# A two-layer decoder trunk: low parts, norms, covers and an overflow body of PE rearranged

## The reference

```python
for l in range(DEPTH):                        # DEPTH = 2
    mod = (c_act @ ada_w[l] + ada_b[l]).reshape(bsz, 6, 1, D_MODEL)
    sh1, sc1, g1, sh2, sc2, g2 = (mod[:, i] for i in range(6))
    h = rms_norm(x, norm1_g[l]) * (1.0 + sc1) + sh1
    y = even_mixer(h, ...) if l % 2 == 0 else odd_mixer(h, ...)
    x = x + g1 * y
    h = rms_norm(x, norm2_g[l]) * (1.0 + sc2) + sh2
    x = x + g2 * grouped_moe(h, router_w, router_b, moe_w_gu[l], moe_w_down[l])
return rms_norm(x, final_g)
```

## Time and profile before

| | us |
|---|---|
| median of three runs | 891.27 (889.9 to 895.1) |
| the profiled execution, its own time | 894.63 |
| its span | 892.8 |
| PE busy | 810.5 (91%) |
| DVE busy | 329.5 (37%) |
| ACT busy | 166.6 (19%) |
| POOL busy | 26.0 (3%) |
| mean DMA rate over the span | 329 GB/s |

### The profile page before, as it was taken

How to read it: one execution, slowest core, us unless ns; L and a number is a source line. 1 busy time by engine, 2 the same in 40 slices (tenths; PEclk the granted TensorE clock), 3 DMA queues, 4 the chain that set the end, 5 groups by cost and what they waited for, 6 DMA issues and landing times.

```text
span 892.8 us, 12085 instructions
## 1 busy us (share of the span) xinstructions
PE 810.5 (91%) x5014; PEld 413.3 (46%) x5014; DVE 329.5 (37%) x815; ACT 166.6 (19%) x397; POOL 26.0 (3%) x65
## 2 busy tenths in 40 slices
PE   4899999899999999866999999898999999999864
PEld 2476444454333333222868778764454333332221
DVE  1188542472121111102789565535482111111102
ACT  2041231511111010002101333432421111010001
POOL 2000010110000000000000000000020000000000
PEclk9999999999999999988999999999999999999978
DMA  9999997687799999999999425202967799999993
GB/s 348 389 363 388 386 364 312 275 316 275 296 431 422 427 423 430 424 423 392 386 345 327 154 95 190 95 1 74 431 262 302 290 430 422 429 422 429 425 423 159
DMA packets 65116, 294.08 MB, mean 329 GB/s; under 512 B 2720, under 2 KB 3360, under 8 KB 49184
## 3 DMA queue, kind: packets, MB, share of 16 engines
q1 hardware_dynamic: 64352, 290.62, 82.1%
q10 hardware_dynamic: 560, 2.10, 0.6%
q0 software_dynamic: 144, 0.52, 0.2%
HBM read 292.18 MB, written 1.05 MB: 328 GB/s over the span
## 4 chain that ended last, share of the span: by engine, by line
PE 52%; issue 24%; DMA 12%; DVE 5%; ACT 3%; SPq 3%; POOL 0%; DVEq 0%; POOLq 0%; ACTq 0%
PE bank L847 13%; PE bank L843 11%; PE bank L1087 9%; DMA ring<-w_gu_dram 6%; PE bank L1109 4%; DMA ring<-w_down_dram 3%; DMA ring<-ada_w_dram 3%; PE bank L1073 3%; SPq L511 2%; PE bank L735 2%; PE bank L1124 2%; PE bank L694 2%; PE bank L759 1%; PE bank L914 1%; ACT tail L1287 1%
## 5 line engine op out<-in xcount | busy, mean ns | idle before, releaser
L1087 PE MATMUL bank<-ring,scr 128*64 128x512 f32 (+1 forms) x1024 | 193.8, 620 | 27.1 <-DMA ring<-w_gu_dram 14.7
L847 PE MATMUL bank<-hT,ring 128*128 128x256 f32 x640 | 142.1, 381 | 0.8 <-DVE hT L1634 0.8
L847 PEld LDWEIGHTS bank<-hT,ring 128*128 128x128 f32 x640 | 120.5, 190 | 18.4 <-issue 1.5
L1087 PEld LDWEIGHTS bank<-ring,scr 128*64 128x64 f32 (+1 forms) x1024 | 56.1, 130 | 151.7 <-issue 128.3
L1109 PE MATMUL bank<-ring,scr 128*64 128x512 f32 (+1 forms) x544 | 102.4, 597 | 1.4 <-DMA ring<-w_down_dram 1.0
L2059 DVE TENSOR_TENSOR hT<-bank,gb 128x512 f32<-128x512 f32 x28 | 19.4, 692 | 190.3 <-PE bank L1109 190.3
L843 PE MATMUL bank<-ring,xh 128*128 128x512 f32 x128 | 58.7, 612 | 0.7 <-ACT xh L1287 0.7
L843 PE MATMUL bank<-ring,hT 128*128 128x512 f32 x128 | 57.7, 607 | 0.1
L1472 ACT ACTIVATE scr<-bank 128x256 f32<-128x256 f32 (+1 forms) x42 | 19.1, 455 | 205.9 <-PE bank L1098 119.6
L1124 PE MATMUL bank<-hT,scr 64*128 64x512 f32 x224 | 55.6, 615 | 1.8 <-DVE hT L2059 1.8
L1109 PEld LDWEIGHTS bank<-ring,scr 128*64 128x64 f32 (+1 forms) x544 | 29.3, 127 | 59.8 <-issue 57.6
(11 more groups left out here) (252 smaller groups left out, 679.6 us busy)
## 6 DMA issues: line engine op xcount, KB each, us to landing
ring<-w_gu_dram SPq DMA_DIRECT2D x60, 2048.0 KB, 19.7
ring<-w_down_dram SPq DMA_DIRECT2D x28, 2048.0 KB, 17.5
ring<-ada_w_dram SPq DMA_DIRECT2D x24, 2048.0 KB, 15.9
ring<-od_w_in_dram SPq DMA_DIRECT2D x9, 2048.0 KB, 16.1
ring<-ev_w_in_dram SPq DMA_DIRECT2D x5, 2048.0 KB, 19.6
ring<-w_down_dram SPq DMA_DIRECT2D x8, 1024.0 KB, 27.3
scr<-w_gu_dram SPq DMA_DIRECT2D x10, 512.0 KB, 6.4
ring<-ev_w_out_dram SPq DMA_DIRECT2D x2, 2048.0 KB, 17.7
```

What stands on the lines that cost most here:

```text
L847: ins = pe.matmul(banks[h][:, m * 256:(m + 1) * 256], w[:, c, (2 * h + m) * P:(2 * h + m + 1) * P], x_part[:, c, :], start=(c == 0 and m = ...
L1087: ins = pe.matmul(b[o:o + r, :].rearrange("p (u f) -> p u f", u=2), h[:, c, r * i:r * i + r], wm, start=(first and c == 0), stop=(last and ...
```

## The change

Five edits.

- The low parts move from POOL to DVE, behind DVE's copy of `modp`. The copy of the router sums moves from DVE to ACT, behind the second high part; that high part moves in front of the exponential, and the first in front of ACT's rows of `hT`.
- The normalised rows are written in two halves of 512 columns on both engines, with a semaphore step for each; PE waits for the second half only in front of its third bank.
- In norms 1 to 3 DVE takes chunks 0, 1, 4, 5 (banks 0 and 2) and ACT chunks 2, 3, 6, 7 (banks 1 and 3).
- PE reads the flag before block 11 of the experts. The identity products are 5 and 7 in the routes, where they were 9 and 8. The four in front of the transposes of `ph` 2 are gone, and five stand behind the last scatter of layer 0, in front of the jump.
- The inside of PE's overflow body is a loop of four turns instead of four copies.

```diff
@@ gpsimd @@
-            def low_part(l):
-                for t in range(T):
-                    pool.wait_ge(hi_ready, 2 * l + t + 1)
-                    pool.tensor_tensor(by_chunks(x_lo[:, t, :]), by_fours(xh[:, t, :]),
-                          by_chunks(x_hi[:, t, :].bitcast(F32)), ALU.subtract)\
-                        .then_inc(lo_ready, 1)
-
             for n in range(5, 9):
                 root(n)
-                if n in (5, 8):
-                    low_part(n // 8)
@@ tensor, norm_T @@
-                if ph == 2:
-                    keep_busy(4, bank[0])
...
-                pe.wait_ge(xh_ready, ph + 1)
-                pe.wait_ge(xh_dve, ph + 1)
                 for b in range(4):
+                    if b % 2 == 0:
+                        pe.wait_ge(xh_ready, 2 * ph + b // 2 + 1)
+                        pe.wait_ge(xh_dve, 2 * ph + b // 2 + 1)
@@ tensor, fill @@
+                    if p == 0 and l == 0 and c >= 4:
+                        pe.wait_ge(hT_act, c - 3)
                     if p == 0 and l == 1 and c == 0:
-                        pe.wait_ge(hT_dve, 12)
-                    if p == 0 and c >= 4:
-                        pe.wait_ge(hT_act, 8 * l + c - 3)
+                        pe.wait_ge(hT_dve, 10)
+                        pe.wait_ge(hT_act, 10)
+                    if p == 0 and l == 1 and c >= 4:
+                        pe.wait_ge(hT_act if c // 2 % 2 else hT_dve, 8 + 2 * (c // 4) + c % 2 + 1)
@@ tensor, route @@
-                keep_busy(9 - l, bank[0])
+                keep_busy(5 + 2 * l, bank[0])
@@ tensor, experts @@
                 for b in range(BLOCKS):
+                    if b == BLOCKS - 3:
+                        pe.wait_ge(flag_ready, l + 1)
+                        over = pe.value_load(flag[0:1, l:l + 1])
...
                 scatter(BLOCKS - 1)
-
-            def overflow(l):
-                pe.wait_ge(flag_ready, l + 1)
-                over = pe.value_load(flag[0:1, l:l + 1])
+                if l == 0:
+                    keep_busy(5, bank[0])
+                return over
+
+            def overflow(l, over):
                 with pe.If(over > 0):
                     pe.wait_ge(tail_free, 4 * (l + 1))
                     with pe.Fori(0, POS) as e:
                         d = e * 28
-                        for q in range(4):
-                            pe.wait_ge(ov_dve[l], d + (7 * q + 2))
+                        with pe.Fori(0, 28, 7) as q:
+                            at = d + q
+                            pe.wait_ge(ov_dve[l], at + 2)
...
@@ scalar, norm @@
-                act.activation(xh[:, 0, :], xs[:, 0, :], ACT.Copy, scale=rstd[:, 0:1]).then_inc(xh_ready, 1)
+                for j in range(2):
+                    act.activation(xh[:, 0, j * W:(j + 1) * W], xs[:, 0, j * W:(j + 1) * W], ACT.Copy,
+                                   scale=rstd[:, 0:1]).then_inc(xh_ready, 1)
                 l, s = ph // 2, ph % 2
-                if ph == 1:
-                    row_out(2)
+                if s == 1:
+                    act.wait_ge(xh_ready, 2 * ph + 2)
+                    high_part(0)
                 act.wait_ge(x_ready, ph + 1)
-                for c in range(4, 8):
+                for c in ((2, 3, 6, 7) if ph else range(4, 8)):
...
                 if s == 1:
+                    if ph == 1:
+                        row_out(2)
+                    act.wait_ge(xh_dve, 2 * ph + 2)
+                    high_part(1)
+                    act.wait_ge(router_part, l + 1)
+                    act.activation(router_sum, bank[6][:, 0:2 * P], ACT.Copy).then_inc(router_out, 1)
 
                     act.activation(sm(895, 1), ones[:, 0:1], ACT.Exp)
-                    high_part(0)
@@ scalar, route @@
                 act.activation(pr, lg, ACT.Exp).then_inc(pr_ready, 1)
-                high_part(1)
@@ vector, tile_1, hT_rows and norm @@
-                dve.tensor_scalar(xh[:, 1, :], xs[:, 1, :], rstd[:, 1:2], None, ALU.mult).then_inc(xh_dve, 1)
+                for j in range(2):
+                    dve.tensor_scalar(xh[:, 1, j * W:(j + 1) * W], xs[:, 1, j * W:(j + 1) * W], rstd[:, 1:2], None,
+                                      ALU.mult).then_inc(xh_dve, 1)
...
-                for c in range(4):
+                for c in ((0, 1, 4, 5) if ph else range(4)):
...
                     dve.tensor_copy(modp[:, l, :], bank[6][:, 256:272]).then_inc(modp_out, 1)
-                    dve.wait_ge(router_part, l + 1)
-                    dve.tensor_copy(router_sum, bank[6][:, 0:2 * P]).then_inc(router_out, 1)
+                    for t in range(T):
+                        dve.wait_ge(hi_ready, 2 * l + t + 1)
+                        dve.tensor_tensor(by_chunks(x_lo[:, t, :]), by_fours(xh[:, t, :]),
+                          by_chunks(x_hi[:, t, :].bitcast(F32)), ALU.subtract)\
+                           .then_inc(lo_ready, 1)
```

16 lines of the change are left out of this document (8 added, 8 removed).

## The result

Over 15 runs each, the kernel before took 894.33 us and the changed one 887.03 us (medians). The ratio is 0.9917 with a 95% interval of 0.9895 to 0.9940, so the change takes off 7.4 us (5.4 to 9.4). One run of the kernel before took 1224.54 us, which doesn't move its median.

A forecast was written before the change was run, and what follows sets the result against it. PE (TensorE) was taken as the bound, busy 810.5 of 892.8 us, each gain carrying to the end. Border 7.1, route 0 2.6 and route 1 1.4 sum to 11.1: 891.3 to 880.2 us, range 875.5 to 886.5.

The forecast's parts named there:

- Border: Between the layers, norm 2: the first projection product starts 7.1 us sooner.
- a jump of 0.6: Border: PE's jump over the smaller overflow body costs 0.6 us, where a gap of 4.84 stood.
- 2.2 from transposes to projection: Norm 2: first transpose to first projection product takes 2.2 us instead of 2.76, as DVE and ScalarE share the chunks.
- The chosen reading: Border: the gap of 4.84 us comes from the overflow body's size; 184 instructions instead of 736 bring it to 0.6.
- the rival with 18%: Border: the jump keeps its 4.84 us, gain there about 1.5 instead of 7.1, time 885.8 us; chance 18%.
- Route 0: Route of layer 0: stall beside GpSimd gone, PE's shorter identity products end at 185.35 instead of 187.99, gain 2.6 us.
- the bound of -1.5: Route of layer 0: gain of -1.5 us if the adaLN row before the identity products is at half clock too.
- Route 1: Route of layer 1: DVE's stall of 2.87 us goes, first reduce 1.5 later, identity products covered; gain 1.4 us.
- its bound of 0.3: Route of layer 1: gain only 0.3 us if the clock loss of layer 0 occurs here.
- At nothing: Halves in norm 0, flag read before block 11 and layer 0's earlier front load: counted as no gain or loss.
- Slower rival: Routes and border: shortened identity products leave gathers and first projection at 1.2 GHz, together +11 us, 902 us; chance 3%.
- The stall's cause: Routes: GpSimd's low parts hold up tiny DVE operations, 5.24 us for two in layer 0; moving them removes it.

The follow-up runs named there:

- e2: Kernel before with only the border's edits (flag read ahead, five products behind the scatter, none before the transposes, body as a loop): 889.34 us, ratio 0.9950.
- e4: Changed kernel with the border edits taken back; halves, low parts on DVE and shorter covers stay: 894.85 us, ratio 1.0011.
- e9: Kernel before with only PE's flag read three blocks earlier; overflow body still written out four times: 892.16 us, one execution, against 893.61.
- e10: e9 with the overflow body as a loop over its four blocks: 890.38 us, one execution, against 893.61.
- e3: e2 with the overflow body written out four times, as in the kernel before: 888.53 us, ratio 0.9947.
- e5: Kernel before, unchanged, timed against itself and profiled a second time: 893.62 us against 893.01, ratio 0.9998.
- e1: Changed kernel with whole rows instead of halves in norm 0: 885.83 us against 893.33 for the kernel before, ratio 0.9925.
- e16: Changed kernel, unchanged, profiled a third time: 887.58 us, one execution, against 893.94 for the kernel before.
- e13: Changed kernel with five identity products in route 0 and four instead of seven in route 1: ratio a little under the expected 0.989 to 0.991.
- e11: Changed kernel with one and four identity products in the routes instead of five and seven; route 1 took 19.05 us, layer 0's experts lost 5.3.
- e12: e8 with one and four identity products in the routes instead of five and seven; experts of layer 0 took 232.24 us.
- e14: Changed kernel with three and four identity products in the routes instead of five and seven: ratio 0.4% under the changed kernel's 0.9917; route 0 took 21.71 us.
- e8: Changed kernel with the low parts on GpSimd again, each as soon as its high part is there: 886.49 us against 893.01, ratio 0.9928.

## Why the prediction was right at the border and failed in the routes

**Border: right by the stages.** The forecast was 7.1 us, the stages show 7.3 in the mean (5.9 to 8.5, by which profile of before is taken) and 7.38 in the two first profiles. By timing, these edits alone give 4.5 (e2), and on top of the rest, from e4 to the changed kernel, 8.4. Its parts: a jump of 0.6 (measured nothing, hidden behind the products), first half rows as the new limit, 2.2 from transposes to projection (measured 2.36, 422.52 - 420.16). Halves and the split of the chunks are worth the difference of 4.74 (e2) to 3.86, 0.9 us, where the forecast's 2.76 - 2.2 had 0.6 for the split alone. The ten products were as long as forecast (4.56, forecast 4.3). That the panel isn't late next held too: the projection's 64 products run without a break. DVE does wait 3.35 us for the second adaLN panel at 432.34, which holds up nobody on PE.

**The jump's cause: right.** The chosen reading (a body of 184 is near the small ones) is borne out by e9 and e10, and the rival with 18% falls. What the working lacked is that the cover makes it moot: the rival priced 885.8 for a jump of 4.84 behind the products, and e3 with just that body and the products in front of it lost nothing, because the sequencer runs ahead of the engine. The border's sum would have held with the large body too.

**Route 0: the step that failed.** "With the same loss of 1.95, ten passes take 6.25: 185.35 instead of 187.99, **2.6 us**." DVE's side was right: low part 2.04 (estimate 2.2), the pair 0.38 (0.4), the selection 2.9 us sooner (2.46). PE's side was mis-sized: the identity products were to start 12.6 us after the root (179.1), and start at 14.6 in the first profile of the changed kernel and at 15.0 in the other two. The sum took over the adaLN row at full clock, 1.92, and it takes 3.64 in all three; the picks before it take 1.00 instead of 0.59. The prediction had this only as the bound of -1.5. What the sum lacked is that the new order itself leaves PE idle for longer in front of the picks, and that in ten of eleven profiles the clock is lower behind that than it was in any of before.

The time compared with, 21.52 after the root, was the long end of what before shows, too: e5 and e2 have 20.3, e3 has 19.8. The gain over the means is 0.4 instead of 2.6. PE was 0.2 to 1.9 us behind the selection before, and is 1.8 (e1) to 4.6 us (e16) behind it now, so nearly all that DVE gained is lost in waiting for PE.

The first profile of the changed kernel hides this. Its counting products come 19.00 us after the root, where the forecast had 18.9. That is luck: they start their cover 2.0 us late, and the ten passes happen to take 4.56 instead of 6.25.

**Route 1: the same kind of error.** The selection came 1.7 us sooner relative to the root (forecast 1.4). But "from 648.8 end at 654.8, before the selection" failed: the fourteen passes took 7.97, 8.23 and 8.37 instead of 6.0, and PE became the bound, by 1.1 to 2.2 us. The working had the price of this as its bound of 0.3. In this route before has such stretches too, in four of its seven profiles, but not in the one that was read. The gain is 0.7 instead of 1.4. The counterpart is e13, whose eight passes leave the selection as the bound at 19.05, 2.5 us under the mean of before.

**At nothing: held.** Halves in norm 0 cost nothing that shows (e1), nor does the flag read ahead: experts 0 take 226.13 us with it and 226.08 without, and the chain of waits of the changed kernel hangs on the same transfer as the earlier trace rows:

```profile
346.70 29.55 DMA ring<-w_gu_dram
```

**Slower rival: its mechanism exists, at another size.** Gathers at 1.2 GHz behind a cut cover cost 5.3 us in e11's experts, the number that it had priced for route 0 and its gathers together. That the two are equal is chance, since e11's route itself is shorter. By one profile each of e11, e12 and e14 it sets in somewhere between three products and one, and the change has five. The rival asked what the shortened products do to the clock; that the reordering in front of them costs clock, nobody had priced.

**The stall's cause.** GpSimd beside DVE was the cause, as assumed; the conclusion that DVE must therefore do the work was not needed (e8). The Trainium skill, "SBUF — State Buffer", section "SBUF: two separate sides", describes the lock; 5.24 us beside GpSimd against 0.38 agrees. e8 adds that a low part of GpSimd costs DVE 0.09 us when all but its last 0.3 us falls where DVE waits for PE or runs the four short operations in front of the pair, which keep their 0.17 to 0.19 us.

**The sum.** 7.1 + 2.6 + 1.4 became 7.3 + 0.4 + 0.7 by the stages. What was lost of the gain is the two routes, in both because the working took the clock of one profile of before for that of the changed kernel. What was lost of the time is this and the starting point: from the profiled run of before (894.63), which the prediction had at hand, the same sum gives 883.5.

**Open.** What in the new order of route 0 lowers the clock; why one product there doesn't bring it back where three do; why route 1 forgives four; the 2 us between e2's timed gain and its stages; why e2 and e4 together give 3.5 us and the whole 7.4; whether covers of 5 and 4 or 3 and 4 beat the changed kernel.

## What to carry to other kernels

Put work whose result nobody waits for between the last real product and a jump: here the sequencer crossed even the large body behind 4.56 us of it, and the body written as a loop needed no cover at all. When an operation is made early on another engine, ask first when it runs and only then where. When work moves in front of something that TensorE waits for, price the products behind the longer wait at the lower clock: here such products took back most of what VectorE gained. And take a term that lies on TensorE from several profiles of the same kernel before a gain of 2 us is forecast from it: selection times repeated within 0.02 us, TensorE's ends moved by 2.

## What was unexpected of the hardware

- A taken jump on PE over a body of some 736 instructions cost 4.36 us with nothing queued before it (e9; 4.84 to 6.47 with the flag read just before it), none that shows with 4.56 us of products queued (e3), and none over some 184 (e10).
- The identical kernel has stages that differ by up to 4.7 us (even mixer 166.44 to 171.10), through stretches granted 1.2 GHz that fall at other places, while its whole time stays within about 1% (881.38 to 890.30).
- In route 0 the reordering brought the granted clock of the 20 us behind the root from 0.91 or more (seven profiles) to 0.70 to 0.83 (ten of eleven).
- GpSimd and DVE side by side: 5.24 us for two operations of 128x16 when both want to run, 0.47 when GpSimd has started its second part 2.6 us ahead of them (173.79 against 176.35, e8).
- The low part with its stride of four took DVE 2.04 us against 1.22 in line, a ratio of 1.67; ScalarE's is 1.80 (2.07 against 1.15).
